# Layer two's attention with its tokens in two tiles of 128 consecutive tokens, ordered by residue inside each tile

## The reference, cut to what matters

```python
DILATED_GROUPS = ((128, 1), (512, 4), (2048, 16))     # (window, dilation)
rel = Q_BLOCK + i - m
band = (rel >= 0) & (rel <= w_sub)                    # causal, at most window/dilation steps back
bias = rel_bias[relative_bucket(rel * dilation)]
s = einsum(q, k) * scale + bias ; s = where(valid, s, NEG_INF)
lse = logsumexp(s) ; p = exp(s - lse) ; o = einsum(p, v)
...
wts = softmax(lse over the 3 groups) ; o = sum(wts * o) ; return o @ w_o
```

## Time and profile before

| what | us |
|---|---|
| median of 3 runs | 772.78 |
| the runs | 772.66 to 773.12 |
| the profiled execution, its own time | 771.64 |
| its span in the trace | 770.0 |

### The profile page before, as it was taken

One profiled execution on the slowest core, in us unless ns is written; L12 is line 12 of the kernel. 1 busy time (PEld: TensorE's weight loads), 2 busy tenths in 40 slices (PEclk: granted clock), 3 DMA queues, 4 the chain that ended last, 5 costly groups with the idle time before them and its releaser, 6 DMA issues.

```text
span 770.0 us, 12712 instructions
## 1 busy us (share of the span) xinstructions
PE 761.4 (99%) x4495; PEld 655.3 (85%) x4495; DVE 503.9 (65%) x674; ACT 397.5 (52%) x536; POOL 113.2 (15%) x173
## 2 busy tenths in 40 slices
PE   9999999999999999999999999999999999999996
PEld 7999977888888888999889898898888888888885
DVE  5788987675455455878667668668647755554543
ACT  4766667453343343855665666556645434333421
POOL 3000001610000000314325235233002000000000
PEclk9999999999999999999999999999999999999998
DMA  8635585785654554659686685684643856556502
GB/s 250 185 106 160 190 247 191 232 263 196 214 190 163 176 192 123 169 150 230 171 221 152 163 232 136 161 237 163 217 137 112 298 170 205 172 195 210 194 1 55
DMA packets 157441, 139.16 MB, mean 181 GB/s; under 512 B 6616, under 2 KB 147008, under 8 KB 157408
## 3 DMA queue, kind: packets, MB, share of 16 engines
q1 hardware_dynamic: 153440, 131.55, 55.1%
q0 software_dynamic: 3712, 6.88, 4.8%
q10 hardware_dynamic: 256, 0.30, 0.1%
HBM read 137.60 MB, written 1.11 MB: 180 GB/s over the span
## 4 chain that ended last, share of the span: by engine, by line
PE 95%; DVE 1%; ACT 1%; DMA 1%; issue 0%; DVEq 0%; POOLq 0%; SPq 0%; POOL 0%; ACTq 0%
PE ps L1165 21%; PE ps L1167 20%; PE ps L1166 20%; PE ps L1416 10%; PE ps L1418 5%; PE ps L1171 2%; PE ps L1173 2%; PE ps L1172 2%; PE ps L1474 1%; PE ps L1330 1%; DMA raw<-in_w_qkv_a 1%; PE ps L1444 1%; PE ps L1483 1%; PE ps L1218 1%; PE ps L1260 1%; PE ps L1186 1%
## 5 line engine op out<-in xcount | busy, mean ns | idle before, releaser
L780 DVE TENSOR_TENSOR w_lo<-raw,w_hi 128x2048 fp32r<-128x2048 f32 (+2 forms) x144 | 279.4, 1956 | 45.9 <-ACT w_hi L500 44.2
L500 ACT ACTIVATE w_hi<-raw 128x2048 fp32r<-128x2048 f32 (+2 forms) x144 | 232.6, 1636 | 51.0 <-DMA raw<-in_w_kv_b 20.7
L1165 PE MATMUL ps<-w_hi,xt 128*128 128x512 f32 x352 | 139.6, 397 | 0.0
L1167 PE MATMUL ps<-w_hi,xt 128*128 128x512 f32 x352 | 137.5, 391 | 0.0
L1166 PE MATMUL ps<-w_lo,xt 128*128 128x512 f32 x352 | 137.2, 390 | 0.0
L665 ACT ACTIVATE work<-ps,stat 128x256 f32<-128x256 f32 x44 | 20.9, 476 | 199.4 <-PE ps L1167 199.4
L1165 PE MATMUL ps<-w_hi,ot 128*128 128x512 f32 x240 | 95.0, 396 | 0.4 <-DVE w_lo L780 0.4
L1167 PE MATMUL ps<-w_hi,ot 128*128 128x512 f32 x240 | 93.6, 390 | 0.0
L1166 PE MATMUL ps<-w_lo,ot 128*128 128x512 f32 x240 | 93.6, 390 | 0.0
L1167 PEld LDWEIGHTS ps<-w_hi,xt 128*128 128x128 f32 x352 | 66.1, 188 | 13.9
L1165 PEld LDWEIGHTS ps<-w_hi,xt 128*128 128x128 f32 x352 | 66.2, 188 | 13.5 <-issue 0.6
(11 more groups left out here) (148 smaller groups left out, 1245.3 us busy)
## 6 DMA issues: line engine op xcount, KB each, us to landing
raw<-in_w_gate_up SPq DMA_DIRECT2D x88, 512.0 KB, 4.8
raw<-in_w_kv_b SPq DMA_DIRECT2D x96, 256.0 KB, 3.9
raw<-in_w_down SPq DMA_DIRECT2D x22, 1024.0 KB, 4.9
raw<-in_w_q_b SPq DMA_DIRECT2D x48, 256.0 KB, 4.1
raw<-in_w_qkv_a SPq DMA_DIRECT2D x23, 512.0 KB, 4.9
raw<-in_w_o_a SPq DMA_DIRECT2D x4, 1024.0 KB, 6.8
work<-bias_rows POOLq DMA_DIRECT2D x64, 64.0 KB, 3.6
raw<-in_w_o_b SPq DMA_DIRECT2D x4, 1024.0 KB, 5.3
```

What stands on the lines that cost most here:

```text
L500: act.activation(w_hi[:, s % CUT, 0:size(s)], raw[:, s % RAW, 0:size(s)], ACT.Copy).then_inc(hi_made, 1)
L780: dve.tensor_tensor(w_lo[:, c, 0:n], raw[:, s % RAW, 0:n], w_hi[:, c, 0:n].bitcast(F32), ALU.subtract).then_inc(lo_made, 1)
L1165: mm(out, xs[0], ws[0], start=start, stop=False)
L1167: return mm(out, xs[1], ws[0], start=False, stop=stop)
```

## The change

The tokens of layer two stand in two tiles of 128 consecutive tokens, and inside a tile by residue: place 32 r + m of tile t holds token 128 t + 4 m + r. Then tile 0's queries have no keys in tile 1. Their scores have 128 columns of group 0 and 32 for each dilated group, 192 in all; tile 1's have 256 and twice 64 (two blocks of 32 keys for each group), 384 in all. `HR` is 32, `OWN` is 64 and 128, `WB` is 192 and 384, `WS` 576.

What follows from it in the code: `every` of tile 0 has 128 columns in place of 256. `own` goes by 4 runs of 32 places, 32 matmuls with 64 rows and 32 queries, of 32 keys for tile 0 and of 64 for tile 1. A head has 5 transposes in place of 6, one of them 64 columns wide. `outputs_b` takes 256 columns for the keys of tile 0 and 128 for those of tile 1, and then 16 matmuls of 32 columns in place of 8 of 64, with 64 rows for tile 0 and 128 for tile 1. `value_b` has 9 ACT instructions for a tile in place of 4, eight of them on 32 partitions. `head_bias` has 12 DMAs and 4 additions in place of 6 and 2. The exponential, maximum and normalization of tile 0 work on 192 columns in place of 384; `transposed_b` copies 640 columns in place of 768. The output leaves in 16 DMAs of 32 rows in place of 8 of 64: SP issues eight for tile 0 and four for tile 1, ACT the other four. The reload of x has 4 DMAs as before. The copy of layer one's attention output into `ot` (`cut_ot`) reads the same elements in another order.

```diff
-WB = SEQ + (NG - 1) * RUN
+HR = P // R
+OWN = [(NG - 1) * HR * (t + 1) for t in range(NT)]
+WB = [P * (t + 1) + OWN[t] for t in range(NT)]
+WS = sum(WB)
...
-    token = R * (np.arange(SEQ) % RUN) + np.arange(SEQ) // RUN
+    place = np.arange(SEQ)
+    token = P * (place // P) + R * (place % HR) + place % P // HR
...
 def store(queue, t, half, r):
-            queue.dma_start(by_residue(out[0])[2 * t + r][:, cols], xn[RUN * r:RUN * r + RUN, t, cols]
+            queue.dma_start(by_residue(out[0])[r, t][:, cols], xn[HR * r:HR * r + HR, t, cols]
...
                     sp.wait_ge(x_made, 6 * NT + 2 * t + half + 1)
-                    store(sp, t, half, 0)
-                    if t == 0:
-                        store(sp, t, half, 1)
+                    for r in range(R - 2 * t):
+                        store(sp, t, half, r)
...
 def head_bias(b, h):
+                    for t in range(NT):
+                        pool.dma_start(band[at_, t].rearrange("p (c n) -> p c n", c=R),
+                                       bands[r][ds(h, 1)][:, :, t].rearrange("h m c n -> (h m) c n")).then_inc(band_in, 16)
+                    pool.dma_start(own_band[at_], own_bands[ds(h, 1)].rearrange("h m t n -> (h m) t n")
...
+                for t in range(NT):
+                    pool.tensor_tensor(to[0], blocked[0], distances[:, 0:t + 1], ALU.add)
+                    inst = pool.tensor_tensor(to[1], blocked[1], distances[:, 0:t + 1].broadcast_to(
+                        [P, t + 1, NG - 1, HR]), ALU.add)
...
 def value_b(p, j, t):
-                act.activation(v[even, 0:2], src[even, 0:2], ACT.Copy, scale=x_rs(2, t)[even])
-                act.activation(v[odd, 0:3:2], src[odd, 0:3:2], ACT.Copy, scale=x_rs(2, t)[odd])
-                act.activation(v[odd, 1], src[even, 2], ACT.Copy, scale=x_rs(2, t)[even])
-                act.activation(v[even, 2], src[odd, 1], ACT.Copy, scale=x_rs(2, t)[odd]).then_inc(vb_made, 1)
+                act.activation(vb[p % 2][:, t, :], src[:, 0], ACT.Copy, scale=x_rs(2, t))
+                for r in range(R):
+                    tokens = slice(HR * r, HR * r + HR)
+                    for g in range(1, NG):
+                        row = HR * (2 * t + g - 1)
+                        inst = act.activation(vown[p % 2][row:row + HR, r], src[tokens, g], ACT.Copy,
+                                              scale=x_rs(2, t)[tokens])
+                inst.then_inc(vb_made, 1)
...
 def scores_b(a, j):
-                        mm(bank(2 + 2 * hh + t, at_, SEQ), qb[r, 0, P * t:P * t + P], kb[r, 0, :],
+                        mm(bank(2 + 2 * hh + t, 0, P * (t + 1)), qb[r, 0, P * t:P * t + P], kb[r, 0, 0:P * (t + 1)],
...
-                    for run in range(2):
-                        tokens, to = slice(P * t + RUN * run, P * t + RUN * run + RUN), slice(RUN * run, RUN * run + RUN)
+                    for run in range(R):
+                        to = slice(HR * run, HR * run + HR)
+                        tokens = slice(P * t + HR * run, P * t + HR * run + HR)
                         for hh, r in enumerate(heads):
-                            inst = mm(bank(2 + 2 * hh + t, at_ + RUN * (g - 1), RUN)[to, :], qb[r, g, tokens],
-                                      kb[r, g, tokens], start=True, stop=True, skip_group_check=True)
+                            inst = mm(out_[:, :, g - 1], qb[r, g, tokens], keys[:, 0:t + 1, to],
+                                      start=True, stop=True, skip_group_check=True)
...
 def transpose_b(a, j, hh):
-                    for n in range(3):
+                    for n in range(t + 2):
+                        first, width = TURNED[0 if n == 0 else 1 if n <= t else 2 + t], OWN[t] if n > t else P
+                        inst = pe.transpose(ps[0:width, at_:at_ + P],
+                                            prob[hh][:, WB[0] * t + P * n:WB[0] * t + P * n + width], eye[:, :])
...
 def outputs_b(a, j):
+                        mm(bank(7, P * kt, SEQ - P * kt)[DH * hh:DH * hh + DH, :], vb[a % 2][:, kt, DH * hh:DH * hh + DH],
+                           turned[hh][:, TURNED[kt]:TURNED[kt] + SEQ - P * kt], start=kt == 0, stop=False,
+                for t in range(NT):
+                    for r in range(R):
+                        for hh in range(2):
+                            inst = mm(bank(7, P * t + HR * r, HR)[DH * hh:DH * hh + DH, :],
+                                      vown[a % 2][0:OWN[t], r, DH * hh:DH * hh + DH],
+                                      turned[hh][0:OWN[t], TURNED[2 + t] + HR * r:TURNED[2 + t] + HR * r + HR],
```

More of the change, by code:

```diff
@@ L73, in shape_constants @@
     square = np.stack([eye, later, strict, np.ones((P, P), np.float32)], 1)
-    token = R * (np.arange(SEQ) % RUN) + np.arange(SEQ) // RUN
-    own = RUN * (i[:, None] // RUN) + np.arange(RUN)[None, :]
-    every = np.broadcast_to(np.arange(SEQ)[None, :], (P, SEQ))
+    place = np.arange(SEQ)
+    token = P * (place // P) + R * (place % HR) + place % P // HR
+    own = HR * (i[:, None] // HR) + np.arange(HR)[None, :]
     parts = []
-    for t, g, keys in ((0, 0, every), (0, 1, own), (0, 2, own), (1, 0, every)):
-        window, dilation = GROUPS[g]
-        dist = token[P * t:P * t + P, None] - token[keys]
-        seen = (dist >= 0) & (dist % dilation == 0) & (dist // dilation <= window // dilation)
-        parts.append(np.where(seen, 0.0, OUTSIDE))
-    parts.append(np.zeros((P, NG * 2 * P - SEQ - WB)))
+    for t in range(NT):
+        blocks = [(0, np.broadcast_to(place[None, :P * (t + 1)], (P, P * (t + 1))))]
+        blocks += [(g, P * u + own) for u in range(t + 1) for g in range(1, NG)]
+        for g, keys in blocks:
+            window, dilation = GROUPS[g]
+            dist = token[P * t:P * t + P, None] - token[keys]
+            seen = (dist >= 0) & (dist % dilation == 0) & (dist // dilation <= window // dilation)
+            parts.append(np.where(seen, 0.0, OUTSIDE))
     mask = np.concatenate(parts, 1).astype(np.float32)
@@ L457, in _ @@
+                inst.then_inc(bias_made, 1)
             pool.memset(expo[:, :], -0.5).then_inc(expo_made, 1)
@@ L771, in _ @@
                 act.wait_ge(x_made, 8 * NT - 1 + half)
-                store(act, NT - 1, half, 1)
+                for r in (2, 3):
+                    store(act, NT - 1, half, r)
         @block.vector
```

101 lines of the change are left out of this document (51 added, 50 removed).

## The result

The changed kernel takes 775.41 us (median; 775.06 to 777.24) beside 772.72 for the kernel before on the same chip. The ratio is 1.0040, with a 95% interval of 1.0030 to 1.0051: slower by 2 to 4 us. The forecast was slower by 9.9, to 782.7. The direction came out, the size did not.

A forecast was written before the change was run, and what follows sets the result against it. PE was taken as the bound, waiting for nothing in layer two's attention. Eight pairs at +1.00 us (8.0), 0.1 for ACT in the first pair and 1.8 for the stores gave +9.9, to 782.7 us; range 773 to 792.

The forecast's parts named there:

- own scores: PE, `own`: 128 instructions in place of 64, eight parts together, most fed at 8 ns: +0.30 us a pair.
- transposes: PE, `transpose_b`: one transpose fewer a head, but the 64-column one adds two changes of shape: +0.38 us a pair.
- own outputs, rounds: PE, own part of `outputs_b`: 16 rounds in place of 8, each staying 0.058 us: +0.46 us a pair.
- own outputs, change to 64 rows and back: PE, `outputs_b`: tile 0's 64-row part between full-height ones adds two changes of shape: +0.30 us a pair (0 to 0.40).
- a change of shape costs 0.15 to 0.20: PE's small matmuls: remainders of 0.15 to 0.20 us come wherever the shape of the array part changes.
- The bound of -0.109 a head: PE, `transpose_b`: low bound for a head, if the narrow transpose's two changes of shape are free.
- priced at 784.4: PE, narrow transposes: if float32 transpose mode is barred they take two passes, 0.11 a head, 1.7 in all: 784.4 us.
- rival 2: PE: narrow transposes free, short rounds in `outputs_b`, rest as forecast; only the stores left, about 774.6 us; chance 0.18.
- The stores: Tail behind PE: SP issues 12 in place of 6, each 467 to 596 ns whatever its bytes: +1.8 us.
- ACT's cost of 0: ACT, `value_b`: nine instructions add 1.6 us a tile, just covered in a step by ACT's idle time: 0.
- POOL's cost of 0: POOL, `head_bias`: a head goes to about 14 us, two to 28 of a 30.8 us step, still covered: 0.
- Rival 4: POOL becomes the bound: twelve small DMAs land in 6 us, PE's six loop steps wait about 1.8 each: 794; chance 0.04.

The follow-up runs named there:

- the second (775.98 and 772.45): The unedited changed kernel run again as a control beside the kernel before, with a second profile: 775.98 us, ratio 1.0044 (1.0030 to 1.0058).

## Why the prediction was right or wrong

PE's terms for a pair, by the chain of each kernel:

| term | forecast | measured |
|---|---|---|
| scores over every key | -0.22 | -0.21 |
| own scores | +0.30 | +0.12 |
| transposes | +0.38 | -0.22 |
| outputs over every key | -0.22 | -0.21 |
| own outputs, rounds | +0.46 | +0.44 |
| own outputs, change to 64 rows and back | +0.30 | +0.27 |
| sum | +1.00 | +0.19 |

The step that failed is the transposes'. The forecast read "a change of shape costs 0.15 to 0.20" from four places in the earlier trace rows, and put it on a narrow instruction between full ones. All four places were changes in which a smaller part meets others beside it; none was a single narrow transpose in a row of full ones, and there the charge was zero. Why it was zero there, and 0.13 to 0.20 us a change elsewhere, no run tells. The bound of -0.109 a head was in the text, and was the value. That is 0.60 of the 0.81 us too much for a pair, 4.8 us in all. For the same transposes the Trainium skill's page "TensorEngine Tiling (Array Packing)", section "Restrictions", would have them barred by column tiling, which the forecast priced at 784.4; the rows show them on parts of 128 by 64, in one pass each (16 narrow loads for 16 heads), at no price, and the measurement decides.

The own scores were mis-sized: 0.74 us in place of 0.92. The eight parts ran together, and 128 instructions were fed at a mean of 5.8 ns. The forecast had feared 8 ns for the larger part of them. 0.18 for a pair, 1.4 us.

The own outputs were right in both terms. The reading that a round is set by the 64 weight columns decided this, and the runs with 8 moving columns (0.88) and with 32 weight columns (0.69 with twice the instructions, 0.51 without the change of shape) bear it out; rival 2, half rounds for half the columns, falls.

The stores were wrong, +1.8 forecast and 0 measured by the kernel before with sixteen of them. The failed step is that an issue takes the times of the earlier trace rows "whatever its bytes": with 32 rows it took 425, and the landing took 1.7 to 1.9 us in place of 2.4 to 2.9, which the forecast had carried over from the earlier trace rows unchanged. The two savings pay for the longer queue.

Transposes, own scores and stores account for 8.0 of overestimate (4.8 + 1.4 + 1.8). From 9.9 they leave 1.9, and the steps measured 1.5. What the forecast did not have at all is +1.3 of PE's wait in the last step and +0.9 at the end. ACT's cost of 0 rested on the cover in a middle step, where PE needs the values only at its second block; the last step has no such block in between, and there ACT's copy of weights stood ahead of the values and waited for a piece that landed late. POOL's cost of 0 rested on 28 us against a step of 30.8. Both numbers were off: a head took 15.2 us in the mean, not 14, and the step was 29.96 because PE did better than forecast. The head shown above has the forecast's 14, its twelve issues at 7.0 us where 7.2 were forecast; in other heads the wait for the landing was up to 6.4 us in place of 3.8. So POOL crossed over from waiting to being late, though by so little that in another execution of the same code (14.8 us a head) it did not. Rival 4 named the place, and gave it 0.04 at 794; what came of it was not PE waiting for biases in six steps but bias DMAs drifting into the stretch where the output weights arrive. That the 0.9 at the end goes with twelve DMAs is shown by the profiles of all kernels but one: 7.5 us behind PE's last matmul in all eight with twelve, 6.4 to 6.7 in the nine others. The exception is the kernel with stores of 64 rows: twelve DMAs, and the interval is 0.16 us as before. Why it comes and goes is not shown.

The three parts, 1.5, 1.3 and 0.9, are 3.7 us. The medians differ by 2.7 in the first comparison and by 3.5 in the second (775.98 and 772.45). Executions without the wait would explain a lower median, but no profile of the unedited kernel shows one.

The forecast had called itself wrong below 29.9 us a step, and the step is 29.96: on the edge, with the mechanism in half of its terms and the size in none of the sum. The range of 773 to 792 held the time because rival 2 (774.6) kept it open below, though that rival's reason, short rounds, was not the one that came true; its free transposes were.

## What to carry to other kernels

Take the price of a switch from rows where the same two shapes meet in the same way, and where there is none, put the whole of it into the range and nothing into the sum. When an engine off the critical path gets longer in a loop, compare its time for an iteration with the new length of the iteration, not the old: once it is over, its lead is used up without a trace in the middle, and it shows in the last iteration, where its transfers meet others. And count small matmuls by the larger of their weight and data columns, since halving the smaller of the two buys nothing.

## What the runs showed of the hardware that was not expected

- A matmul round on side-by-side parts takes 0.9 to 1.0 ns for each column of weights or data, whichever are more: 55 to 58 ns for 64 weight columns with 8 to 64 moving ones, 32 for 32 by 32 (where the feeding may set it), 56 for 32 by 64.
- A single transpose of 64 columns among full ones: 0.55 us for the five, narrow or full.
- A store whose rows are 2 groups of 32 runs on 2 DMA engines (16 small packets for 8 stores, 256 for 16 plain ones; at most 3 packets in flight), and the tail behind PE is 24.1 us in place of 7.5.
- A store issue of 32 rows takes 425 ns on SP, one of 64 rows 564.
- POOL issued a load 3.4 us after its release in all five kernels with eight bias DMAs a head that left it to POOL, and 0.3 us after it in eleven others; the cause is open.
- After 4.3 us without work PE ran at 0.64 of its clock over 4 us, which made the wait cost 5.9. After 1.7 us without work it ran at 0.50 (1.2 GHz) for 3.4 us in one profile. In the profiles with waits of 1.3 and 1.6 us it stayed at full clock.
- A weight piece of 1 MB landed in 4.7 to 5.0 us where the last bias DMA had been issued 5 us or more before it, and in 6.6 to 7.9 where one was issued 1 us before it or later.
